# A third buffer for the raw weight tiles of the first input projection, with the shift transfers requested behind the tiles

## The reference

```python
h = rms_norm(x, g_mix)                    # [256, 1024]
y = h @ w_in                              # w_in is [1024, 2208]
# columns 0..415: latent attention (rank 256 query, rank 128 key/value, 32 rotary)
# the others: r, k, v (512 each) and three small groups of 256 together, of the recurrent part
prev = jnp.pad(feat, ((0, 0), (1, 0), (0, 0)))[:, :-1]     # feat: the 1792 recurrent columns of y
feat = feat + (prev - feat) * mu          # every token mixed with the token before it
```

## Time and profile before

| what | value |
|---|---|
| three runs | 1049.13, 1050.56, 1053.37 us |
| median | 1050.56 us |
| span of the profiled execution | 1050.0 us |
| PE busy | 967.3 us, 92% of the span |
| DVE, ACT, POOL busy | 587.3, 479.8, 123.3 us |
| DMA, mean over the span | 218 GB/s, 228.68 MB |
| `first_in` | from 0 to about 82.5 us of the span |

### The profile page before, as it was taken

How to read it: one execution, slowest core, us unless ns; L and a number is a source line. 1 busy time by engine, 2 the same in 40 slices (tenths; PEclk the granted TensorE clock), 3 DMA queues, 4 the chain that set the end, 5 groups by cost and what they waited for, 6 DMA issues and landing times.

```text
span 1050.0 us, 20505 instructions
## 1 busy us (share of the span) xinstructions
PE 967.3 (92%) x8706; PEld 693.3 (66%) x8706; DVE 587.3 (56%) x933; ACT 479.8 (46%) x822; POOL 123.3 (12%) x142
## 2 busy tenths in 40 slices
PE   6899999998756678999999999999999999999996
PEld 5676896554333344887658777776986648777774
DVE  5577888611000004799766554564988856545543
ACT  5566652410000005665664545446657765453442
POOL 5510550000000001014010000000033410000000
PEclk9999999999888899999999999999999999999999
DMA  8756119899999997765044665663725033757611
GB/s 260 228 163 217 43 43 366 341 403 420 421 421 421 421 414 243 261 221 176 26 166 155 207 213 169 218 217 144 235 95 161 2 121 132 242 170 237 217 64 41
DMA packets 108747, 228.68 MB, mean 218 GB/s; under 512 B 7305, under 2 KB 86203, under 8 KB 94075
## 3 DMA queue, kind: packets, MB, share of 16 engines
q1 hardware_dynamic: 105691, 219.38, 57.9%
q0 software_dynamic: 2976, 8.14, 2.7%
HBM read 224.63 MB, written 1.05 MB: 215 GB/s over the span
## 4 chain that ended last, share of the span: by engine, by line
PE 63%; DMA 13%; DVE 9%; ACT 3%; issue 1%; POOL 1%; SPq 1%; DVEq 0%; POOLq 0%
PE later_pB L924 20%; PE later_pB L933 10%; DMA ring<-in_w_down 9%; PE later_pB L880 4%; PE later_pB L384 4%; DMA wt<-in_w_down 3%; PE rw_pB L1404 2%; PE rw_pB L1425 2%; DVE field L298 2%; PE later_pB L912 2%; PE rw_pB L2476 1%; DMA wt<-in_ev_w_in 1%; PE rw_pB L1433 1%; PE later_pB L4059 1%; PE rw_pB L2242 1%
## 5 line engine op out<-in xcount | busy, mean ns | idle before, releaser
L924 PE MATMUL later_pB<-field 128*128 128x256 f16 x1920 | 212.9, 273 | 0.0
L924 PEld LDWEIGHTS later_pB<-field 128*128 128x128 f16 x1920 | 187.7, 98 | 25.6
L753 DVE SCALAR_TENSOR_TENSOR field<-field 128x2048 f16<-128x2048 f32 x84 | 153.8, 1869 | 56.8 <-ACT field L648 56.8
L648 ACT ACTIVATE field<-field 128x2048 f16<-128x2048 f32 x84 | 126.4, 1567 | 15.5 <-DMA field<-in_ffn_w_up 9.2
L933 PE MATMUL later_pB<-field 128*128 128x512 f16 x528 | 117.7, 379 | 0.6 <-DVE field L753 0.6
L384 PE MATMUL later_pB<-field 128*128 128x256 f16 (+2 forms) x960 | 114.9, 274 | 0.6
L384 PEld LDWEIGHTS later_pB<-field 128*128 128x128 f16 x960 | 94.2, 99 | 13.5 <-ACT field L320 1.8
L933 PEld LDWEIGHTS later_pB<-field 128*128 128x128 f16 x528 | 51.6, 98 | 58.8 <-issue 1.5
L1404 PE MATMUL rw_pB<-ring,kept 128*32 128x256 f32 x816 | 64.9, 409 | 25.0 <-DMA ring<-in_w_up 21.9
L1336 DVE TENSOR_TENSOR rw_mu_a<-rw_pB,rw_mu_a 128x256 f32<-128x256 f32 x8 | 3.4, 425 | 119.6 <-PE rw_pB L1404 119.6
L1404 PEld LDWEIGHTS rw_pB<-ring,kept 128*32 128x32 f32 x816 | 35.6, 118 | 50.0 <-issue 36.1
(11 more groups left out here) (592 smaller groups left out, 1594.3 us busy)
## 6 DMA issues: line engine op xcount, KB each, us to landing
ring<-in_w_up SPq DMA_DIRECT2D x26, 1024.0 KB, 26.6
ring<-in_w_gate SPq DMA_DIRECT2D x25, 1024.0 KB, 21.7
ring<-in_w_down SPq DMA_DIRECT2D x23, 1024.0 KB, 26.4
field<-in_ffn_w_down SPq DMA_DIRECT2D x22, 1024.0 KB, 5.0
field<-in_ffn_w_gate SPq DMA_DIRECT2D x20, 1024.0 KB, 7.6
field<-in_ffn_w_up SPq DMA_DIRECT2D x20, 1024.0 KB, 9.9
wt<-in_ev_w_in SPq DMA_DIRECT2D x9, 1024.0 KB, 5.7
wt<-in_od_w_in SPq DMA_DIRECT2D x9, 1024.0 KB, 5.6
```

Source lines behind the costliest of these rows:

```text
L648: copy = lambda o, i, scale=1.0: nc.scalar.activation(o, i, ACT.Copy, scale=scale)
L753: return nc.vector.scalar_tensor_tensor(out, whole, scale, hi, ALU.mult, ALU.subtract)
L924: ins = T.matmul(p[:, s, j * SEQ:(j + 1) * SEQ], w[:, s, m, c, j::NJ], h[:, c, :], start=(n == 0), stop=(n == 3 * KC - 1))
```

## The change

The projection gets an optional third raw buffer, and `first_in` passes it `ahead`. Tile k now lies in buffer k % 3: `wt[0]`, `wt[1]`, `ahead`. The third buffer has a semaphore of its own, `third_in`. ACT and DVE read the tile through `raw(k)`, and ACT waits for what `raw_in(k)` names. SP requests tile k once `lo_ready` counts k - 2 instead of k - 1, tile 2 with no wait at all, and within a turn of the loop the shift now follows the tile instead of preceding it.

```diff
+    def raw(self, k):
+        n = self.tiles[k][1]
+        if self.third is None:
+            return self.wt[:, k % 2, :, 0:n]
+        return self.third[:, :, 0:n] if k % 3 == 2 else self.wt[:, k % 3, :, 0:n]
+
+    def raw_in(self, k):
+        if self.third is None:
+            return self.w_in[k % 2], 16 * (k // 2 + (self.first is None and self.late is None))
+        return (*self.w_in, *self.third_in)[k % 3], 16 * (k // 3 + (k % 3 == 2))
...
-            act.wait_ge(self.w_in[k % 2], 16 * (k // 2 + (self.first is None and self.late is None)))
+            act.wait_ge(*self.raw_in(k))
...
                     for k in range(2, n_tiles):
                         at, n = FIRST_TILES[k]
+                        if k > 2:
+                            sp.wait_ge(pr.lo_ready, k - 2)
+                        sp.dma_start(pr.raw(k), wv[:, :, at:at + n]).then_inc(pr.raw_in(k)[0], 16)
                         if k - 4 in shift_of:
                             shift(k - 4)
-                        sp.wait_ge(pr.lo_ready, k - 1)
-                        sp.dma_start(pr.wt[:, k % 2, :, 0:n], wv[:, :, at:at + n]).then_inc(pr.w_in[k % 2], 16)
...
-                    first_in(nc, con, x, w, m, wt, tokens(a["x"][0]), ...
+                    first_in(nc, con, x, w, m, wt, ahead.rearrange("p (c n) -> p c n", c=KC), tokens(a["x"][0]), ...
```

More of the change, by code:

```diff
@@ L226, with __init__ @@
              "moved", "norm_link"]
-    def __init__(self, nc, name, ctx, con, src, gain, w, tiles, y, first, late=None, rooms=None, ready=None, psum=None, gcol=None):
+    def __init__(self, nc, name, ctx, con, src, gain, w, tiles, y, first, late=None, rooms=None, ready=None, psum=None, gcol=None,
+                 third=None):
         sb = lambda n, s, d=F32: ctx.enter_context(nc.sbuf_tensor(f"{name}_{n}", s, d))
@@ L233, in __init__ @@
         self.wt, self.first = first
+        self.third, self.third_in = third, []
         big = max(n for _, n in tiles)
@@ L287, in high_part @@
         else:
-            act.wait_ge(self.w_in[k % 2], 16 * (k // 2 + (self.first is None and self.late is None)))
+            act.wait_ge(*self.raw_in(k))
             if k >= 2:
                 act.wait_ge(self.product, k - 1)
-        self.nc.scalar.activation(self.w_hi[:, k % 2, :, 0:n], self.wt[:, k % 2, :, 0:n], ACT.Copy,
-                                  scale=W_SCALE).then_inc(self.hi_ready, 1)
+        self.nc.scalar.activation(self.w_hi[:, k % 2, :, 0:n], self.raw(k), ACT.Copy, scale=W_SCALE).then_inc(self.hi_ready, 1)
     def low_part(self, dve, k):
@@ L297, in low_part @@
         dve.wait_ge(self.hi_ready, k + 1)
-        self.nc.vector.scalar_tensor_tensor(self.w_lo[:, k % 2, :, 0:n], self.wt[:, k % 2, :, 0:n], W_SCALE,
+        self.nc.vector.scalar_tensor_tensor(self.w_lo[:, k % 2, :, 0:n], self.raw(k), W_SCALE,
                                             self.w_hi[:, k % 2, :, 0:n], ALU.mult, ALU.subtract).then_inc(self.lo_ready, 1)
@@ L1576, in shifted, with first_in @@
         return [(p[1:SHIFT + 1], f[0:SHIFT]), (p[SHIFT + 1:P], f[SHIFT:P - 1]), (p[0:1, 1, :], f[P - 1:P, 0, :])]
-def first_in(nc, con, x, w, m, wt, tokens, shift_in, low, marks, positions, identity, late):
+def first_in(nc, con, x, w, m, wt, third, tokens, shift_in, low, marks, positions, identity, late):
     W0, A0, K_K = range(3)
@@ L1586, in first_in @@
         sb = lambda n, s, d=F32: ctx.enter_context(nc.sbuf_tensor("fi_" + n, s, d))
-        pr = Projection(nc, "in1", ctx, con, x, w["g_mix"], w["w_in"], FIRST_TILES, m.feat, (wt, None), rooms=m.rooms)
+        pr = Projection(nc, "in1", ctx, con, x, w["g_mix"], w["w_in"], FIRST_TILES, m.feat, (wt, None), rooms=m.rooms, third=third)
         gains, tables = sb("gains", [P, 2, MLA_QK]), sb("tables", [P, 2, TT, 4, 16])
@@ L1607, in first_in @@
                 "g_out", "q_made", "q_out", "q_squared", "k_made", "v_made", "k_squared", "v_out", "qn_turned", "qn_out",
-                "norms", "roots", "gains_ready", "vlink", "glink", "base_split"] + [f"shift{j}" for j in shift_of]
+                "norms", "roots", "gains_ready", "vlink", "glink", "base_split", "third_in"] + [f"shift{j}" for j in shift_of]
         with Stage(nc, "in1", Projection.NAMES + side) as sems:
@@ L1613, in first_in @@
              cq_out, ckv_out, lora_out, lora_done, sig_ready, a_ready, g_done, g_out, q_made, q_out, q_squared, k_made, v_made,
-             k_squared, v_out, qn_turned, qn_out, norms, roots, gains_ready, vlink, glink, base_split) = \
+             k_squared, v_out, qn_turned, qn_out, norms, roots, gains_ready, vlink, glink, base_split, third_in) = \
                 sems[len(Projection.NAMES):len(Projection.NAMES) + len(side) - len(shift_of)]
+            pr.third_in = [third_in]
             pr.late = LateInputs((x0_in, x1_in), identity_in, (tile0_in, tile1_in), early_set, squared)
@@ L4198, in hybrid_kernel @@
                     late = {n: (t, a[n]) for n, t in (con | more).items() if n != "identity"}
-                    first_in(nc, con, x, w, m, wt, tokens(a["x"][0]), arrived_of["shift"], low, marks, a["positions"], a["identity"], late)
+                    first_in(nc, con, x, w, m, wt, ahead.rearrange("p (c n) -> p c n", c=KC), tokens(a["x"][0]), arrived_of["shift"], low, marks, a["positions"], a["identity"], late)
                     views.append(layer1.enter_context(nc.sbuf_tensor("own_slot", [P, 2 * D], F32))[:])
```

## The result

| | time, us (median; range) | runs |
|---|---|---|
| before | 1049.61 (1047.81 to 1053.37) | 21 |
| after | 1052.22 (1049.47 to 1057.34) | 21 |

The ratio is 1.0029 [1.0019, 1.0039]: the changed kernel is 3.0 us slower (0.0029 x 1049.6), between 2.0 and 4.1. That lies within the 0.5% that I had called no change, and inside the range, but the interval excludes no change, and the forecast of 1050.9 on a median of 1050.56 was +0.3. So the forecast's range held, but its sum did not: most of what happened has to be explained by something else.

The account below looks back on a forecast made before the run. The prediction took PE as pacing the stage, with the low part of tile 3, behind mix(0) and shift 0, deciding its end. Terms 0 + 0 + 0.3 us on the median 1050.56 gave 1050.9; 8-in-10 range 1048.0 to 1054.2.

Parts of the forecast that it names:

- what bounds the stage: In first_in, PE's two holes around tile 3 (3.0 us together) become one; the low part of tile 3 sets the pace.
- the shift: On SP's queue, shift 0 stands behind one more 1 MB tile and lands at 30.0 instead of 29.3, 0.7 us later.
- the count of free DMA time: Idle DMA time from 12 us on absorbs 2.1 of the extra tile's 2.8 us, leaving shift 0 0.7 late.
- the cover of POOL: POOL's last row operation holds mix(0) until 30.3, so shift 0 landing at 30.0 costs nothing.
- the term for POOL itself: The w_uq transfer shares DMA with a larger tile, so POOL's chain ends later: +0.3 us through mix(0).
- The sum through the mix: At mix(0), the shift's delay costs 0 and POOL's later end 0.3: +0.3 us in all.
- rival C: The granted clock falls in the last part of tile 3 after the joined hole: +1.7 us, 1052.6; chance 0.10.
- the signs of the prediction: Wrong if mix(0) begins before 29 or low part makes 31.8 (rival A), or tile 4 starts after 41 (Rival B, D).
- Rival B: The DMA queue absorbs nothing: shift 0 lands 2.8 us later, at 32.1, costing 1.8 us, 1052.4; chance 0.15.
- D: Tile 2's early request delays tiles 0 and 1 at the stage's start by about 1.0 us: 1051.9; chance 0.05.
- rival A: Both PE holes around tile 3 close, with mix(0) 3.0 us sooner: 1047.5; chance 0.08.

Follow-up runs that it names:

- e1: The changed kernel run and profiled again with no edit; 1053.49 us, ratio 1.0037 to before.
- e2: The changed kernel with nine useless filler products on PE ahead of the last 16 products of tile 3; 1051.3 us, ratio 1.0018 to before.
- e3: The changed kernel, third buffer kept, but each shift put back ahead of the tile request; 1048.38 us, ratio 0.9981 to before.
- e5: The kernel before, run and profiled again with no edit; a single run, 1049.05 us.
- e7: The kernel before with only tile 2 requested early into the third buffer, shifts ahead of tile requests; 1051.3 us, ratio 1.0008 to before.
- e11: The changed kernel run and profiled once more with no edit; a single run, 1055.53 us.
- e6: The kernel before, run and profiled once more with no edit; a single run, 1050.12 us.
- e4: The kernel before with one DVE instruction of the stage's tail run twice (0.73 us); 1051.66 us, ratio 1.0013 to before.
- e8: The changed kernel, but with tile 2 requested together with tile 3; 1052.49 us, ratio 1.0028 to before.
- e10: The changed kernel with DVE's low part of tile 3 moved ahead of mix(0); 1049.17 us, ratio 0.9999 to before.
- e12: e3 with DVE's low part of tile 3 also moved ahead of mix(0); 1049.81 us, ratio 1.0007 to before.
- e9: The kernel before, two buffers kept, with only the tile request put ahead of the shift; 1057.13 us, ratio 1.0066 to before.

## Why the prediction came out as it did

**Right: what bounds the stage.** Tile 3 started at 28.34 (28.3 forecast), ACT's waits for weights were gone, the two holes became one ended by DVE, and tiles 5 to 8 and shifts 3 to 7 cost nothing: the stage ends 42.75 us after tile 4 starts in after, e1, e2, e3, e5 and e7, 42.76 in before, and 43.02 in e11, where the clock was still low at tile 4.

**Right in size, by luck in part: the shift.** I gave shift 0 a delay of 0.7 us. The mix began 0.9 us later in the means of four traces each, and the last piece took 6.9 us instead of 6.2 (7.4, 6.1, 5.6, 5.8 before; 6.2, 7.1, 7.6, 6.5 after). But the count of free DMA time stopped at 26, although the shift landed at 29.2. The next stretch of the trace before has more than half of it free, share 0.45:

```profile
26.00:28.00 2.00, 2.00 (x30) 2.00 (x28) 0.00 (x0) 0.15 (x1) 2.00 (x1) 1.00 0.45 102
```

With its 1.1 us (2 x 0.55) the count is 3.2 us, more than the 2.8 of the tile, and the delay would have been 0. The shift was still under way while the engines were half idle in the mean, so free time in the mean is not what decides when it lands. What fits the small delay is e7 and e3: before and after alike, one tile goes out just ahead of the shift, tile 3 or tile 4.

**Wrong: the cover of POOL.** The step read "a shift that lands at 30.0 therefore costs nothing", since POOL's last operation held the mix until 30.3. That cover was a feature of the trace. Of the four it is in before and, on the second instruction (2.54 us), in e6. In e5 and e4 POOL was done at 27.72 and 27.81, before the shift landed, nothing was held, and a delay of the shift counts in full. And the term for POOL itself, 0.3 for a later `w_uq`, was too small: its last operation ended 1.5 us later in the mean (30.6 against 29.1). Most of that is `w_uq`: POOL's first operation starts at 20.8 in the mean before and at 22.0 after. In two traces of four on each side one of POOL's operations was held by DVE (3.69 and 3.64 us before, 3.98 and 4.05 after, 2.8 elsewhere), which cancels. The sum through the mix was forecast as +0.3; the means of four give +1.2, with the spread named above.

**Wrong: the odds of rival C.** I gave the fall of the clock 0.10, and priced it at 1.7. It came in all three traces of the changed kernel, and in e8, and costs 1.57 us in after (6.41 - 4.84), 1.51 in e1 and 3.84 in e11. The mean of the three is 2.3. With the 1.2 this makes 3.5 us, and the timed runs say 3.0 (2.0 to 4.1) and, in e1, 3.9 (1.9 to 5.8). What I had not weighed is how easily a joined hole falls: it was 2.12, 3.71 and 3.94 us where I had reckoned with 3.3, and the smallest of them was enough. So C should have been likelier than not. By the signs of the prediction the later runs count against it as well: tile 4 started after 41 in e1 (41.98) and e11 (44.35), though by C and not by B or D, to which that sign was given.

The Trainium skill, page "TensorE: Matmul & The Clock Gate", section "Why this matters for your kernels", says that a long enough hole between bursts of products puts the array back to its lower clock. The traces agree (five joined holes of 2.12 us and more, five falls), and the row of e10 shows that one long hole is not the only way there.

**Wrong: what the old order was worth.** The 7.4 us of shift 0's landing I took as a queue that the change makes a little longer. That the same piece lands after 2.6 us when no tile is requested within 5 us ahead of it (e3) was not in my sum; I compared the new order with the old and not with the one that costs least. The Trainium skill, page "DMA: Bandwidth & Descriptors", section "Queues, rings and completion order", says that a completion is written only behind every earlier write of that DMA engine; the 2.6 and 6.2 us agree.

**The base.** I laid the change on a trace whose stage ended at 82.55; the others of the same kernel end at 80.65, 81.87 and, less the added 0.73, 80.15. The forecast for the stage's end, 82.8, was nearly that of after (83.27) only because the base was late. Against the mean of the four (81.3) the stage of after, e1 and e11 (mean 85.1) lost 3.8 us: 1.4 up to the last part, 2.3 from there to tile 4, and 0.1 behind it.

**Rival B** (the queue absorbs nothing) did not happen; the mix of the changed kernel began between 29.07 and 29.51, not at 32.1. What rival A describes can be had, both holes closed, but by putting the shift ahead of the tile (e3), not by the change as made.

**Open.** How much of the timed loss is the fall and how much the later mix, which rests on three and four traces; why the fall near 200 us comes and goes; and what, beside the length of the hole, decides the fall at tile 3 to 4: holes of 2.12 us and more always brought it (5 of 5), one of 1.91 (e6) did not, but in e10 it fell where the longest single hole was 1.28, and in e12, with the same products around a hole of 1.03, it did not.

## What to carry to other kernels

Before reordering the requests of a queue, look up which engine waits for each of them: a short transfer that an engine stands waiting for belongs ahead of a long one that is merely early, even if both are issued within a microsecond. When a change moves a hole on PE, look at the length of what the holes become once joined, and price a fall of the clock into the block behind it. And read a cover (a stall that hides a delay) in more than one trace before counting on it.

## What the runs showed of the hardware

- A DVE instruction with two inputs in SBUF and a POOL operation on SBUF can hold each other, both ways: a tensor_tensor of 0.69 us took 1.67, 2.21, 2.50, 2.54 and 2.61 us beside POOL; the scalar_tensor_tensor that writes float16 took 4.00 instead of 2.29 (e3); and POOL's row operations took 4.05 instead of 2.78 (e11) beside DVE's low part of tile 2. Not every overlap does it. DVE's low part of tile 2 started 1.2 us into POOL's first operation in after (22.99; 21.79) and 1.5 us into the second in e5 (24.18; 22.72), both with one input, and neither side was lengthened (1.48 us; 2.78 and 2.80). POOL's last operation, with two inputs, held DVE nearly to its end: in e11 the 0.69 us instruction was done at 31.72, so in effect it began at 31.03, and POOL was done at 31.17.
- A shift piece of 1 KB, issued at nearly the same time, lands after 2.6 us (e3) or 6.2 us (after), depending on whether the 1 MB of the next tile was requested behind it or just ahead of it in the same queue. With any tile just ahead it took 5.6 to 7.7 us where it was issued near 20 us.
- The granted clock fell during idle time, before the next product: in e9 it was 0.82 over 34 to 36 us, a stretch in which PE did nothing, and it stayed at 0.50 well into the block behind:

```profile
34.00:36.00 2.00, 0.00 (x0) 0.00 (x0) 1.82 (x3) 0.89 (x4) 0.00 (x0) 0.82 0.00 0
36.00:38.00 2.00, 0.49 (x3) 0.36 (x4) 2.00 (x4) 0.78 (x3) 0.00 (x0) 0.50 0.00 0
```
